# Summing the adaptive-norm pieces: the first four on TensorE in four column groups, the later ones folded by 32x32 block transposes on VectorE, the gate bias by transfer

## What is computed

```python
cond = jax.nn.silu(c)                                    # one row of 1024
for layer in range(DEPTH):
    mod = (cond @ w_ada[layer] + b_ada[layer])[:, None, :]   # one row of 6 * 1024
    shift_m, scale_m, gate_m, shift_f, scale_f, gate_f = jnp.split(mod, 6, axis=-1)
    hm = _rmsnorm(x, g_mix[layer]) * (1 + scale_m) + shift_m
    x = x + gate_m * _token_mixer(hm, w_in[layer], g_heads[layer], w_out[layer])
    hf = _rmsnorm(x, g_ffn[layer]) * (1 + scale_f) + shift_f
    y = _swiglu(hf, ...) if layer % 2 == 0 else _moe_ffn(hf, ...)
    x = x + gate_f * y
return _rmsnorm(x, g_final)
```

## Time and profile before

| | us |
|---|---|
| median of 3 runs | 1781.99 (1771.41 to 1783.42) |
| the profiled execution, its own time | 1774.51 |
| its span in the trace | 1772.7 |
| PE busy | 1594.6 (90%) |
| DVE busy | 409.1 (23%) |
| ACT busy | 226.2 (13%) |

### The profile page before, as it was taken

The page is one execution under the profiler, slowest core; times in us unless marked ns, Lnnn a source line. Parts: engine busy times, 40 slices in busy tenths (PEclk is TensorE's granted clock), DMA queues, the critical chain, the costliest instruction groups (busy, mean ns, idle before and its releaser), DMA issues.

```text
span 1772.7 us, 19682 instructions
## 1 busy us (share of the span) xinstructions
PE 1594.6 (90%) x8282; PEld 872.2 (49%) x8283; DVE 409.1 (23%) x867; ACT 226.2 (13%) x439; POOL 0.2 (0%) x4
## 2 busy tenths in 40 slices
PE   5999889999989998797597999999999998999975
PEld 5778658777658784432132333334444433333321
DVE  4265523323333633400101002002000110100103
ACT  1122210000011321110011011111011001111101
POOL 0000000000000000000000000000000000000000
PEclk9999899999989998799799999999999999999998
DMA  9955525665745440099999999897666599999995
GB/s 348 326 203 177 190 95 190 237 237 190 262 136 181 167 181 19 3 378 371 342 389 371 382 378 370 327 389 279 248 248 235 208 327 388 370 389 371 389 371 217
DMA packets 168108, 482.18 MB, mean 272 GB/s; under 512 B 10472, under 2 KB 20992, under 8 KB 167936
## 3 DMA queue, kind: packets, MB, share of 16 engines
q1 hardware_dynamic: 168064, 481.57, 74.3%
HBM read 480.49 MB, written 1.05 MB: 272 GB/s over the span
## 4 chain that ended last, share of the span: by engine, by line
PE 74%; SPq 8%; DVE 8%; DMA 6%; issue 3%; ACT 2%; DVEq 0%; ACTq 0%
PE bank L830 14%; PE bank L879 10%; PE bank L640 7%; SPq L527 6%; PE bank L841 6%; PE bank L777 6%; PE bank L826 6%; PE bank L791 4%; DMA ring<-in_w_exp_down 4%; DVE acc L1004 4%; PE bank L759 3%; PE bank L873 3%; PE bank L634 2%; PE bank L962 2%; SPq L533 1%
## 5 line engine op out<-in xcount | busy, mean ns | idle before, releaser
L830 PE MATMUL bank<-ring,hT 128*64 128x448 f32 x1792 | 353.8, 545 | 45.6 <-issue 19.3
L879 PE MATMUL bank<-ring,bt 128*32 128x256 f32 (+1 forms) x1680 | 239.9, 495 | 24.5 <-DMA ring<-in_w_exp_down 12.3
L830 PEld LDWEIGHTS bank<-ring,hT 128*64 128x64 f32 x1792 | 130.0, 137 | 265.9 <-issue 205.9
L1342 DVE TENSOR_TENSOR bt<-bt,bank 128x448 f32<-128x448 f32 (+1 forms) x52 | 32.4, 622 | 807.6 <-PE bank L830 555.0
L879 PEld LDWEIGHTS bank<-ring,bt 128*32 128x32 f32 (+1 forms) x1680 | 86.0, 125 | 160.5 <-issue 119.1
L777 PE MATMUL bank<-hT,ring 128*128 128x256 f32 x704 | 156.0, 383 | 1.2 <-DVE hT L1075 1.2
L640 PE MATMUL bank<-hT,ring 128*128 128x256 f32 x640 | 152.9, 396 | 2.3 <-ACT hT L1424 1.2
L777 PEld LDWEIGHTS bank<-hT,ring 128*128 128x128 f32 x704 | 134.6, 192 | 21.7 <-issue 1.9
L640 PEld LDWEIGHTS bank<-hT,ring 128*128 128x128 f32 x640 | 124.4, 198 | 23.4 <-DVE hT L1075 3.1
L1004 DVE SCALAR_TENSOR_TENSOR acc<-ring,cond,acc 128x512 f32<-128x512 f32 x160 | 120.3, 752 | 5.6
L841 PE MATMUL bank<-ring,hT 128*32 128x448 f32 x1024 | 102.9, 542 | 0.0
(11 more groups left out here) (204 smaller groups left out, 999.8 us busy)
## 6 DMA issues: line engine op xcount, KB each, us to landing
ring<-in_w_exp_gate SPq DMA_DIRECT2D x128, 896.0 KB, 10.4
ring<-in_w_exp_up SPq DMA_DIRECT2D x128, 896.0 KB, 15.1
ring<-in_w_exp_down SPq DMA_DIRECT2D x64, 1536.0 KB, 16.3
ring<-in_w_ada SPq DMA_DIRECT2D x24, 2048.0 KB, 10.4
ring<-in_w_in SPq DMA_DIRECT2D x10, 2048.0 KB, 11.1
ring<-in_w_exp_down SPq DMA_DIRECT2D x64, 256.0 KB, 16.8
ring<-in_w_ff_gate SPq DMA_DIRECT2D x5, 2048.0 KB, 18.6
ring<-in_w_ff_up SPq DMA_DIRECT2D x5, 2048.0 KB, 14.0
```

The lines of the kernel that those rows point to most:

```text
L830: last = mm(o[64 * c2:64 * c2 + 64, 0:EH], xsT[:, k, t0:t0 + 64], w[:, k, c2 * EH:(c2 + 1) * EH], start=(k == 0), stop=(k == KC - 1))
L879: last = mm(bank[4 + 2 * u][m * c:m * c + m, 0:D // parts], hsT[:, u, at_:at_ + m], ed[:, t, c * (D // parts):(c + 1) * (D // parts)], sta ...
```

## The change

The first four pieces are no longer summed by DVE. `ada_rows` runs eight matmuls per piece with one column of `cond`, repeated 32 times, as weights (128x32) and the slot's rows (128x512) as data; chunk k goes to column group k mod 4 of the array, so `bank[i % 2]` holds four partial sums, each on 32 partitions. DVE copies that bank to SBUF (`ada_copy`), and `ada_early` reduces over partitions with four 128x1 matmuls against one column of a new constant `fold`. The first norm's scaling and transposes are moved between pieces 1 and 2.

For a later shift or scale piece DVE, after its eight steps, transposes `acc` in 32x32 blocks into `bank[2]` and reduces it to `folded` [128, 16]; PE then needs four matmuls with `fold` (128x32) as weights and four columns of data, in place of four 128x128 weight loads. For a gate piece the four bias matmuls go; instead `b_ada` is brought by a transfer that writes one 4 KB row into all 128 partitions of `gates` (512 KB each). DVE adds the product to it in place of the copy. Two of these transfers, for layer 0, are issued after stream load 4 and ahead of `idxq`; the two for layer 1 are issued in the dense stage and in layer 1's attention. The first constants grow by 32 columns.

```diff
-ADA_SPLIT = 6
+EARLY = 4
@@ load
                 if n >= SLOTS:
-                    sp.wait_ge(*released(STREAM[n - SLOTS]))
+                    old = STREAM[n - SLOTS]
+                    sp.wait_ge(*released(old))
+                    if later == [0, 1] and old[0] == "ffg" or later == [1] and old[:2] == ("idxq", 1):
+                        kind = later.pop(0)
+                        sp.wait_ge(x_v, 4 * kind + 4)
+                        gate_bias(1, kind)
@@ stream
+                if n == 4:
+                    gate_bias(0, 0)
+                    gate_bias(0, 1)
@@ PE
+            def ada_rows(i):
+                key = ("ada", 0, i)
+                if i >= 2:
+                    pe.wait_ge(row_c, i - 1)
+                arrived(pe, key)
+                for k in range(KC):
+                    g = k % 4
+                    last = mm(bank[i % 2][32 * g:32 * g + 32, :], cond[:, k:k + 1].to_broadcast([P, 32]),
+                              slot(key, CW)[:, k, :], start=(k < 4), stop=(k >= 4))
+                last.then_inc(row_p, 1)
+            def ada_early(i):
+                pe.wait_ge(row_c, i + 1)
+                if i:
+                    pe.wait_ge(ada_c, i)
+                for t in range(4):
+                    last = mm(bank[2][:, t:t + 1], early[i % 2][:, t * P:(t + 1) * P], fold[:, 0:1], start=True, stop=True)
+                last.then_inc(ada_p, 1)
             def ada(key):
-                if i in GATES:
-                    mm(bank[2][:, :], ones, a, start=True, stop=True)
-                    for t in range(4):
-                        row = l * 48 + 4 * i + t
-                        last = mm(bank[2][:, t * P:(t + 1) * P], ident[:, row:row + 1].to_broadcast([P, P]), rows[:, :],
-                                  start=False, stop=True, skip_group_check=True)
+                if key[2] in GATES:
+                    last = mm(bank[2][:, :], ones, acc[:, :], start=True, stop=True)
                 else:
-                    for t in range(4):
-                        last = mm(bank[2][:, t:t + 1], a[:, t * P:(t + 1) * P], ones[:, 0:1], start=True, stop=True)
+                    for q in range(4):
+                        last = mm(bank[2][32 * q:32 * q + 32, 0:4], fold,
+                                  folded.rearrange("p (t q) -> p q t", q=4)[:, q, :], start=True, stop=True)
@@ PE, order at the start
-            for i in range(4):
-                ada(("ada", 0, i))
+            ada_rows(0)
+            ada_rows(1)
+            ada_early(0)
+            ada_early(1)
+            turn(norm_no(0, 0))
+            for i in (2, 3):
+                ada_rows(i)
+                ada_early(i)
@@ DVE, ada_sum
+                        then(ins)
+                        own(ada_c)
+                        then(nc.vector.transpose(bank[2][:, :], acc[:, :]))
+                        signal(nc.vector.tensor_reduce(folded[:, :], bank[2][:, :].rearrange("p (b i) -> p b i", i=32),
+                                                       AX_X, ALU.add), acc_r)
@@ DVE, ada_take
-                    signal(nc.vector.tensor_copy(dst, bank[2][:, :]), ada_c)
+                    ve.wait_ge(s_gbias, 32 + 16 * (kind + 1) * l)
+                    signal(tt(dst, dst, bank[2][:, :], ALU.add), ada_c)
@@ DVE, order at the start
-            ada([("ada", 0, i) for i in range(4)])
+            ada_copy(0)
+            ada_copy(1)
+            ada_take_all(early_keys[:2])
+            norm(0, 0)
+            norm(0, 1)
+            for i in (2, 3):
+                ada_copy(i)
+                ada_take_all(early_keys[i:i + 1])
```

More of the change, by code:

```diff
@@ L62 @@
 ALIBI = 12
-C_IDENT, C_ONES, C_TRIU, C_NEGTRI, C_NEGONES, C_SLOT = (i * P for i in range(6))
-C_FIRST = 2 * P
+C_IDENT, C_ONES = 0, P
+C_FOLD = 2 * P
+C_FIRST = C_FOLD + 32
+C_TRIU, C_NEGTRI, C_NEGONES, C_SLOT = (C_FIRST + i * P for i in range(4))
 C_STICK = C_SLOT + T
@@ L246, in constants @@
     ct[:, C_IDENT:C_IDENT + P] = p == j
+    ct[:, C_FOLD:C_FOLD + 32] = p % 32 == j[:, 0:32]
     ct[:, C_TRIU:C_TRIU + P] = p <= j
@@ L290, in build @@
         acc = sb("acc", [P, CW])
+        folded = sb("folded", [P, 16])
         rows = sb("rows", [P, P])
@@ L413, in build @@
         ones = ct[:, C_ONES:C_ONES + P]
+        fold = ct[:, C_FOLD:C_FOLD + 32]
+        early = [acc, arena[:, 0:CW]]
         def slot(key, n):
@@ L486, in source, with gate_bias @@
                 return kview((w_ff_gate if kind == "ffg" else w_ff_up)[0], i * CW, i * CW + n * P), slot(key, n * P)
+            def gate_bias(l, kind):
+                a = (3 * kind + 2) * D
+                sp.dma_start(gates[:, kind, :], b_ada[l:l + 1, a:a + D].to_broadcast([P, D])).then_inc(s_gbias, 16)
+            later = [0, 1]
             def load(key):
@@ L552, in ada @@
+            def ada_early(i):
[5 more added lines that the diff above has]
+                last.then_inc(ada_p, 1)
             def ada(key):
                 n = ADA_NO[key]
[L555 to L561, removed]
-                    for t in range(4):
-                        for k in range(ADA_SPLIT, KC):
-                            mm(bank[2][:, 4 + t:5 + t], slot(key, CW)[:, k, t * P:(t + 1) * P], cond[:, k:k + 1],
-                               start=(k == ADA_SPLIT), stop=(k == KC - 1))
@@ L566, in ada @@
-                pe.wait_ge(acc_r, n + 1)
-                a = acc[:, :]
-                if i in GATES:
-                    mm(bank[2][:, :], ones, a, start=True, stop=True)
-                    for t in range(4):
-                        row = l * 48 + 4 * i + t
-                        last = mm(bank[2][:, t * P:(t + 1) * P], ident[:, row:row + 1].to_broadcast([P, P]), rows[:, :],
-                                  start=False, stop=True, skip_group_check=True)
-                else:
-                    for t in range(4):
-                        last = mm(bank[2][:, t:t + 1], a[:, t * P:(t + 1) * P], ones[:, 0:1], start=True, stop=True)
+                pe.wait_ge(ada_c, n)
@@ L607, in _ @@
             nc.tensor.transpose(bank[4][:, P:P + 24], rows2[:, :], ident[0:24, 0:24]).then_inc(setup_t, 1)
-            for i in range(4):
-                ada(("ada", 0, i))
+            pe.wait_ge(cond_r, 1)
+            ada_rows(0)
[6 more added lines that the diff above has]
+                ada_early(i)
             for l in range(DEPTH):
-                turn(norm_no(l, 0))
+                if l:
+                    turn(norm_no(l, 0))
                 turned(norm_no(l, 0))
@@ L999, in ada_sum @@
                 n = ADA_NO[key]
-                end = ADA_SPLIT if n < 4 else KC
                 w = slot(key, CW)
-                for k in chunks or range(end):
+                for k in chunks or range(KC):
                     if k:
@@ L1005, in ada_sum @@
                     else:
-                        ve.wait_ge(cond_r, 1)
-                        if n:
-                            ve.wait_ge(ada_p, n)
+                        ve.wait_ge(ada_p, n)
                         arrived(ve, key)
                         ins = ts(acc[:, :], w[:, 0, :], cond[:, 0:1], None, ALU.mult)
-                    if k < end - 1:
+                    if k < KC - 1:
                         then(ins)
-                    else:
-                        signal(ins, acc_r)
+                    elif key[2] in GATES:
+                        signal(ins, acc_r)
+                    else:
+                        then(ins)
[3 more added lines that the diff above has]
+                                                       AX_X, ALU.add), acc_r)
             def ada_take(key):
@@ L1020, in ada_take @@
                 if i in GATES:
-                    if l:
-                        own(x_v)
-                    dst = gates[:, GATES.index(i) // 2, (i % 2) * CW:(i % 2 + 1) * CW]
-                    signal(nc.vector.tensor_copy(dst, bank[2][:, :]), ada_c)
+                    kind = GATES.index(i) // 2
+                    ve.wait_ge(s_gbias, 32 + 16 * (kind + 1) * l)
+                    dst = gates[:, kind, (i % 2) * CW:(i % 2 + 1) * CW]
+                    signal(tt(dst, dst, bank[2][:, :], ALU.add), ada_c)
                     return
@@ L1027, in ada_take @@
                 ins = tt(part, bank[2][:, 0:4], cols[:, l * 48 + 4 * i:l * 48 + 4 * i + 4], ALU.add)
-                if ADA_NO[key] < 4:
-                    then(ins)
-                    ins = tt(part, part, bank[2][:, 4:8], ALU.add)
                 if i // 2 in (1, 4):
@@ L1037, in ada_take, with ada_copy @@
                 signal(ins, ada_c)
+            def ada_copy(i):
+                ve.wait_ge(row_p, i + 1)
+                if i >= 2:
+                    ve.wait_ge(ada_p, i - 1)
+                signal(nc.vector.tensor_copy(early[i % 2][:, :], bank[i % 2][:, :]), row_c)
             taken = [0]
@@ L1093, in _ @@
             own(setup_c)
-            ada([("ada", 0, i) for i in range(4)])
+            early_keys = [("ada", 0, i) for i in range(EARLY)]
+            ada_copy(0)
```

(6 more changed lines are left out.)

2 lines of the change are left out of this document (added).

## The result

| | before | changed |
|---|---|---|
| median, us | 1776.7 (4 runs) | 1902.7 (4 runs) |
| span of the profiled execution, us | 1772.7 | 1900.4 |
| first expert product, us after the start | 749.6 | 753.4 |
| code transfers on queue 8 | 30 | 93 |

The changed kernel takes 1.0727 times the time of the one before (95% interval 1.0677 to 1.0778): 126 us more, where +8.6 was forecast.

The account below looks back on a forecast made before the run. PE, busy 90% of the span, was taken as the bound, DVE mattering only where PE waits. +3.7 - 1.2 + 2.4 - 2.3 + 6.0 = +8.6 us, set on the runs' average 1778: 1786 us, range 1776 to 1796, wide 1770 to 1804.

Parts of the forecast that it names:

- keep their own time, apart from the start they are given: Expert stage: adaptive work exists only before about 600 us, so the experts behind it were given no term.
- No rival of mine: Whole kernel: small gain 1776 (0.25), dear fold 1805 (0.15), serial start 1783 to 1818 (0.05); no change not separate.
- Start: Up to the first projection: +1.7 us for `idxq` behind the bias transfers, +2.0 for slow projection records, together +3.7.
- half clock throughout: Early pieces at the start: `ada_rows` taken at twice its full-clock 1.8 us, 3.7 us a piece.
- Gates: Eight gate pieces in attention and dense stages: 0.89 us less PE time each, 7.1 us in all; take unchanged at 0.68.
- Fold: Later shift and scale pieces: +1.45 us DVE, 0.6 less PE; +0.85 where PE waits, +6.0 in the dense stage.
- The estimate of 1.24 us for the transpose: DVE's 128x512 block transpose: four times the skill's 311 ns; would make the sum 5 us higher.
- The clock: Dense stage: seven PE stalls give 3.5 falls of the granted clock at 1.7 us each, +6.0 us (0 to 11.9).
- The nine stretches of before: Trace of before: stretches with 2.1 to 2.6 us of idleness at full clock; the clock fell after five.
- the case that the prediction drew from the Trainium skill: Dense stage: all seven stalls followed by a clock fall, the sum 6 us higher.
- the dense stage, forecast at +8.4: Dense stage: fold +6.0 less 3.6 from gates, +2.4, and clock falls +6.0.
- Layer 0's attention, forecast at -1.2: Layer 0's attention: two fold pieces that wait +1.7, two that do not -1.1, two gates -1.8.

Follow-up runs that it names:

- 6377: Changed kernel with padding that puts the expert loop at PE instruction 6377, 256 behind 6121: 1780.2 us, ratio 1.0027.
- 6091: Changed kernel with 96 padding instructions, so the expert loop begins at PE instruction 6091: 1781.7 us, ratio 1.0019.
- 6121: Loop's place in the kernel before; changed kernel with 126 waits behind the early pieces puts it there again: 1781.3 us, ratio 1.0016.
- 6180: Changed kernel with the expert loop at PE instruction 6180: 1785.5 us, ratio 1.0044.
- 6144: Changed kernel with the expert loop at PE instruction 6144: 1795.1 us, ratio 1.0121, from 2 runs.
- 5995: The changed kernel without padding, its expert loop at PE instruction 5995: 1902.7 us, ratio 1.0727.
- 6058: Changed kernel with 63 padding instructions at the start, so the expert loop begins at PE instruction 6058: 1902.9 us.
- 6251: Kernel before, none of the change, with 130 more PE instructions behind the setup transposes, loop at 6251: 1904.2 us, ratio 1.0677.

## Why the prediction was wrong

**The step that failed** is the sentence that the experts "keep their own time, apart from the start they are given". It treated stages whose work is untouched as untouched in time. The work was the same, the place of its code was not, and that cost 122 us. The trace of before held the sign of it: a wait of 19.3 us of PE at the first turn, released by nothing the profile shows, and 30 transfers on the code queue, none of them in the later turns. I passed over it as a wait that the change leaves alone. A price could have been put on it: six further turns of 19.3 us are 116 us. No rival of mine had it; the range of 1770 to 1804 and 0.13 for slower came from the adaptive part alone.

The Trainium skill, Runtime: NRT & Kernel Launch, section Instruction fetch mechanics, says that each engine's instructions come in blocks of 16 KiB (256 instructions), that PE holds 2048 of them, and that a taken branch to a target outside the current window of two blocks waits for a transfer. The trace agrees with the block (16.3 KB a transfer), the runs with the period of 256. The window of two blocks is not what these runs show: the loop of the kernel before is 6.7 blocks long and went through all turns but the first without a transfer. The page gives no price; here a turn took 4.5 to 27.1 us in the changed kernel.

**The terms of the sum**, up to the experts: forecast +8.6 us, measured +3.7 at the first expert product.

- *Start.* Right in what decides: the projection is released by `idxq`, not by `hT`. With the transfers ahead of it PE had `idxq` 1.35 to 3.0 us later than with them behind, where 2.7 was forecast; the forecast landing at 47.5 is met within 0.4 us in five of the eight profiles, and the changed kernel's own, at 46.04, is the earliest. `ada_rows` was mis-sized: the first piece took 3.64 us, the others 1.92 to 2.35, for I had kept half clock throughout; nothing hung on it. The slow first projection after the long wait was +1.7 against +2.0. Six wide matmuls in the wait took this away (14.05 us). Narrow ones did not: with the loop at 6377 PE ran matmuls of four columns from 36.6 to 46.6 us, the granted clock was 0.52 in that stretch, and after a wait of only 0.87 us the 64 records took 15.61 us.
- *Gates.* The bias products are gone. The take is an addition of 0.679 us against the copy's 0.684, as forecast.
- *Fold.* The operations measured 0.727 and 0.692 us, 1.50 with the chain's steps, against 1.45. The groups by shape of the changed kernel (count, busy us, mean ns, idle before), and one line of its timeline:

```profile
L1052 DVE STREAM_TRANSPOSE bank<-acc 128x512 f32<-128x512 f32 x12 | 8.7, 727 | 0.4
L1053 DVE TENSOR_REDUCE folded<-bank 128x16 f32<-128x512 f32 x12 | 8.3, 692 | 0.4
```
```profile
306.13 0.24 PE L604 MATMUL bank<-folded,ct 128*32 128x4 f32 x8 [2.11 <-DVE folded L1053]
```

  PE's idle time ahead of the seven products in the dense stage is 1.58 to 2.18 us (2.11 in this line), where 1.6 to 2.1 was forecast; the products take 0.24 where 0.4 was set. Both sides of the trade were right, and so was its sign: undoing the fold gained 5.3 us in the dense stage. The estimate of 1.24 us for the transpose, which the prediction set beside its 0.69, was too high for this form (0.727).
- *The clock.* Mis-sized by all of it: 6.0 us for 3.5 falls in the dense stage, and there were none. Two windows of the changed kernel (busy us of PE, PEld, DVE, ACT, POOL, then PEclk, DMA share, GB/s):

```profile
300.00:350.00 50.00, 46.26 (x195) 33.80 (x193) 20.10 (x33) 1.55 (x5) 0.00 (x0) 1.00 0.84 312
350.00:400.00 50.00, 46.25 (x193) 33.80 (x194) 16.55 (x29) 1.91 (x5) 0.00 (x0) 1.00 0.57 211
```

  PEclk is 1.00 through all seven waits of 1.6 to 2.2 us. The nine stretches of before on which I built a chance were 2.1 us and longer, and only two of the seven waits (2.11 and 2.18) are. Nor did a fall follow every wait, the case that the prediction drew from the Trainium skill, TensorE: Matmul & The Clock Gate, section HAM oscillation — how this bites in real kernels. The waits in the loop described there are longer than these, so the case was not one for these stalls. So the dense stage, forecast at +8.4 with its share of the fold and the gates, took 1.3 us more. Layer 0's attention, forecast at -1.2 and +2.0 for its slow first projection, took 5.7 us more, with the clock at half from 183 to 186 and again from 203 to 220, where it had fallen at 209 before. In other kernels with the same code this stage took 1.3 to 8.6 us more than before; what moves it is open. One term 7 us too high and one 5 us too low: that the sum up to the experts is off by only 5 us is luck.

## What to carry to other kernels

A program with a loop has a cost that no operation in it shows: where the loop lies. When an edit changes the number of instructions ahead of a large loop on an engine, look first at the code queue's transfers and at waits at the turns that nothing released; compare the two kernels at the same place of the loop before judging the edit, and hold the place by padding in time the engine has to spare. Then the parts can be told apart: here the bias transfers and the early pieces on PE together brought the first expert product forward by 6.3 us in one profile, though the whole execution (ratio 0.9956 to 1.0019) does not show it; the fold was not worth keeping, since it put 1.5 us on the engine that PE was waiting for to spare 0.8 on PE.

## What the runs showed of the hardware

- The expert loop of 1705 PE instructions runs with 30 or 31 code transfers in all at four places (6091, 6121, 6180, 6377), with 38 at one (6144), and with 93 or 94 at three others (5995, 6058, 6251), 5 to 11 pieces of 16.3 KB at each of its seven turns.
- In those three a turn costs roughly the more of PE's time, the more of the loop's code lies between the expert just done and the next. The loop holds four bodies in a row, and each expert runs one of them. Behind an expert of the first body the turn took 24.2 to 28.2 us, of the second 14.6 to 24.2, of the third (the one with the products of L863) 4.0 to 4.5. Within the second, it took 14.6 to 18.4 us when the next expert ran the first body, 18.4 to 18.6 the second, 23.0 to 24.2 the third. That the branches over skipped bodies are why was not tried.
- 126 instructions that only wait on semaphores long reached took 12.8 us on PE, 0.1 us each (7.6 us of it showed as idleness when they stood ahead of the expert loop); 31 fp32 matmuls of 128x32 weights and four columns, 124 instructions, took 3.2 us.
- Four column groups with 512 columns took 1.92 us for eight fp32 matmuls at full speed, where L841's rows gave 1.8, and 3.64 us for the first piece, when PE came from idleness.
